# Retention head outputs and gates laid with tokens on partitions, normed per token, then turned

## The reference, cut to what matters

```python
q, k, v, g = split(h @ w_in, [1024, 2048, 4096])      # widths 1024, 1024, 2048, 2048
q, k = rotary(q), rotary(k) * 256 ** -0.5
# per head: scores (256 x 256) times decay ** |distance|, a decay for each direction, times v
o = o_fwd + o_bwd                                      # (token, head, 512)
mu  = mean(o, axis=-1);  var = mean((o - mu) ** 2, axis=-1)
o = ((o - mu) * rsqrt(var + 1e-6)).reshape(b, s, 2048) * gn_g
return (silu(g) * o) @ w_out                           # 2048 -> 1024
```

## Time and profile before

| | us |
|---|---|
| median of three runs | 1710.88 |
| the profiled execution | 1711.01 |
| its span, first to last instruction | 1708.9 |
| PE matmul busy | 1640.0 (96%) |
| PE weight load busy | 1492.4 (87%) |
| DVE busy | 1258.7 (74%) |
| ACT busy | 897.9 (53%) |
| mean granted TensorE clock | 0.982 of 2.4 GHz |
| retention stage, projections, within the trace | 988.9 to 1126.2 |
| retention stage, heads and output chunks | 1126.2 to 1216.4 |

### The profile page before, as it was taken

One profiled execution on the slowest core, in us unless ns is written; L12 is line 12 of the kernel. 1 busy time (PEld: TensorE's weight loads), 2 busy tenths in 40 slices (PEclk: granted clock), 3 DMA queues, 4 the chain that ended last, 5 costly groups with the idle time before them and its releaser, 6 DMA issues.

```text
span 1708.9 us, 28898 instructions
## 1 busy us (share of the span) xinstructions
PE 1640.0 (96%) x10694; PEld 1492.4 (87%) x10694; DVE 1258.7 (74%) x1868; ACT 897.9 (53%) x1165; POOL 42.1 (2%) x50
## 2 busy tenths in 40 slices
PE   8988999989799999999999999998999999799998
PEld 8877999968699999878999998987899997699997
DVE  5765878767688787875877775448787786878777
ACT  5474544554665455564554554444554555555453
POOL 0000000000000000000000042000000000000000
PEclk9999999989899999999999999999999999899999
DMA  7353454434464544422545455522455454445543
GB/s 277 102 181 133 175 193 179 189 126 169 148 246 174 195 176 169 173 100 95 195 170 203 170 178 195 175 96 89 169 195 203 169 191 173 148 148 197 196 172 123
DMA packets 42148, 288.61 MB, mean 169 GB/s; under 512 B 4929, under 2 KB 5057, under 8 KB 8673
## 3 DMA queue, kind: packets, MB, share of 16 engines
q1 hardware_dynamic: 40000, 278.62, 44.6%
q0 software_dynamic: 2080, 9.05, 1.5%
HBM read 286.61 MB, written 1.05 MB: 168 GB/s over the span
## 4 chain that ended last, share of the span: by engine, by line
PE 83%; DVE 10%; ACT 3%; issue 2%; DMA 1%; DVEq 0%; SPq 0%; ACTq 0%
PE bank L1721 15%; PE bank L1723 15%; PE bank L1722 15%; PE bank L1815 7%; PE bank L1816 7%; PE bank L1817 7%; PE bank L1767 3%; PE bank L1769 3%; PE bank L1768 3%; DVE w_lo L989 2%; PE bank L1708 1%; DVE arena L1262 1%; ACT w_hi L533 1%; PE bank L1864 1%; PE bank L1843 1%
## 5 line engine op out<-in xcount | busy, mean ns | idle before, releaser
L1721 PE MATMUL bank<-h_hi,w_hi 128*128 128x256 f32 x2368 | 680.9, 288 | 18.6 <-issue 9.9
L1722 PE MATMUL bank<-h_hi,w_lo 128*128 128x256 f32 x2368 | 674.6, 285 | 0.0
L1723 PE MATMUL bank<-h_lo,w_hi 128*128 128x256 f32 x2368 | 674.6, 285 | 0.0
L1721 PEld LDWEIGHTS bank<-h_hi,w_hi 128*128 128x128 f32 x2368 | 456.2, 193 | 28.1 <-issue 17.5
L1722 PEld LDWEIGHTS bank<-h_hi,w_lo 128*128 128x128 f32 x2368 | 456.3, 193 | 4.6 <-issue 1.4
L1723 PEld LDWEIGHTS bank<-h_lo,w_hi 128*128 128x128 f32 x2368 | 456.2, 193 | 1.0
L989 DVE TENSOR_TENSOR w_lo<-raw,w_hi 128x2048 fp32r<-128x2048 f32 (+3 forms) x119 | 249.1, 2101 | 118.0 <-ACT w_hi L533 117.7
L1289 DVE TENSOR_TENSOR w_lo<-raw,w_hi 128x2048 fp32r<-128x2048 f32 x145 | 327.5, 2285 | 1.6 <-ACT w_hi L729 1.6
L717 ACT ACTIVATE arena<-arena,par 128x256 f32<-128x256 f32 x220 | 120.4, 595 | 357.9 <-DVE arena L1248 354.7
L729 ACT ACTIVATE w_hi<-raw 128x2048 fp32r<-128x2048 f32 x150 | 286.0, 1907 | 19.7 <-PE bank L1817 19.7
L1815 PE MATMUL bank<-w_hi,h_hi 128*128 128x512 f32 x632 | 249.3, 395 | 3.7 <-DVE w_lo L989 2.2
(11 more groups left out here) (184 smaller groups left out, 1296.3 us busy)
## 6 DMA issues: line engine op xcount, KB each, us to landing
raw<-wstream SPq DMA_DIRECT2D x258, 1024.0 KB, 4.8
arena<-window_bias POOLq DMA_DIRECT2D x4, 768.0 KB, 6.8
arena<-dilated_bias POOLq DMA_DIRECT2D x8, 256.0 KB, 3.3
arena<-conv_rows POOLq DMA_DIRECT2D x2, 1024.0 KB, 5.9
raw<-wstream SPq DMA_DIRECT2D x4, 384.0 KB, 3.3
raw<-wstream SPq DMA_DIRECT2D x6, 256.0 KB, 3.1
x<-x_in SPq DMA_DIRECT2D x1, 1024.0 KB, 4.8
raw<-wstream SPq DMA_DIRECT2D x2, 512.0 KB, 6.6
```

What stands on the lines that cost most here:

```text
L1721: nc.tensor.matmul(dst, w_parts[0], x_parts[0], start=start, stop=False, **kw)
L1722: nc.tensor.matmul(dst, w_parts[1], x_parts[0], start=False, stop=False, **kw)
L1723: return nc.tensor.matmul(dst, w_parts[0], x_parts[1], start=False, stop=stop, **kw)
```

## The change

Gates become `token_chunk` products like the values, and `value_evac` applies Silu with the scale per token on ACT; `by_root` and the in-place Silu are gone for them. An output has tokens on partitions. The statistics come from `bn_stats` and `bn_aggr` along the free axis, the root is on 128 x 2 columns, ACT writes `(o - mean) * root` into SBUF, DVE multiplies by the gate, PE transposes the result into the head's two banks (`turn_head`), and ACT and DVE take `h_hi` and `h_lo` from there with the gain. All four heads' decays are computed beside chunks 8 to 11. `mean` and `var` are gone, and the orders of PE, ACT and DVE are new.

```diff
-    for c in range(16, 24):
-        split_hi(c0 + c + 2)
-        g = pair(g_r, c - 16)
-        act.wait_ge(evac_v, k["ev"] + c - 15)
-        nc.scalar.activation(g, g, ACT.Silu).then_inc(evac_done, 1)
+    for c in range(8, 24):                                    # ACT
+        split_hi(c0 + c + 2)
+        if 8 <= c < 12:
+            act.wait_ge(mask_v, 2 * (c - 8) + 2)
+            nc.scalar.activation(d_r[:, c - 8, :], d_r[:, c - 8, :], ACT.Exp).then_inc(mask_a, 1)
+        if c % 2:
+            n = (c - 9) % 8 // 2
+            value_evac(c0 + c - 1, (v_r if c < 16 else g_r)[:, :, n * 512:(n + 1) * 512],
+                       func=ACT.Copy if c < 16 else ACT.Silu)
+    def head_norm(h):
+        act.wait_ge(v_ready, k["v"])
+        nc.scalar.activation(r_y[:, h, :], r_v[:, h, :], ACT.Abs_reciprocal_sqrt).then_inc(ars_done, 1)
+        act.wait_ge(ret_root, h + 1)
+        for j in range(2):
+            nc.scalar.activation(o_tok(h, j), o_bank(h, j)[:, :], ACT.Identity, bias=r_b[:, h, j:j + 1],
+                                 scale=r_y[:, h, j:j + 1]).then_inc(ret_normal, 1)
+    def head_parts(h):
+        for n in range(2):
+            act.wait_ge(ret_turned, 2 * h + n + 1)
+            for t in range(2):
+                slot = 4 * h + 2 * n + t
+                nc.scalar.activation(h_hi[:, slot, :], o_bank(h, n)[:, t * S:(t + 1) * S], ACT.Identity,
+                                     scale=pcol("ret_gn_g_2", slot)).then_inc(hhi_done, 1)
+    split_hi(c0 + 26); head_norm(0); head_norm(1); head_parts(0); head_parts(1); head_norm(2)
+    head_parts(2); split_hi(c0 + 27); head_norm(3); head_parts(3)
+    for c in range(28, 34): split_hi(c0 + c)
...
+    def stats(h):                                             # DVE
+        for j in range(2):
+            dve.wait_ge(ret_out, 2 * h + j + 1)
+            nc.vector.bn_stats(y_st[:, j, h, :], o_bank(h, j)[:, :]).then_inc(ret_stats, 1)
+    def head_root(h):     # two bn_aggr, var + eps, wait for ACT's root, three Newton steps, -mean * root
+    def head_gate(h):
+        for j in range(2):
+            dve.wait_ge(ret_normal, 2 * h + j + 1)
+            nc.vector.tensor_tensor(o_tok(h, j), o_tok(h, j), g_r[:, j, h * 512:(h + 1) * 512], ALU.mult)
+    def head_parts(h):    # four scalar_tensor_tensor: o_bank * gain - h_hi into h_lo
+    for c in range(8, 24):
+        if c < 12: decays(c - 8)
+        split_lo(c0 + c + 2)
+    probs(0); probs(1); stats(0); head_root(0); stats(1); head_gate(0); probs(2); head_root(1)
+    probs(3); head_gate(1); head_parts(0); stats(2); head_parts(1); head_root(2); head_gate(2)
+    split_lo(c0 + 26); stats(3); head_root(3); head_parts(2); head_gate(3)
+    split_lo(c0 + 27); head_parts(3)
+    for c in range(28, 34): split_lo(c0 + c)
...
+    def output(h):                                            # PE
+        pe.wait_ge(prob_done, 4 if h == 3 else h + 1)
+        for j in range(2):
+            for jt in range(2):
+                at = jt * S + j * P
+                last = nc.tensor.matmul(o_bank(h, j)[:, :], p_r[:, h % 2, at:at + P],
+                                        v_r[:, jt, h * RVD:(h + 1) * RVD], start=jt == 0, stop=jt == 1)
+            last.then_inc(ret_out, 1)
+    def turn_head(h):     # waits ret_gated 2h + 2; eight transposes, ret_turned after each four
+    score(0); score(1); output(0); output(1); score(2); score(3); turn_head(0); output(2)
+    turn_head(1); output(3); project(0); project(1); turn_head(2); project(2); project(3)
+    turn_head(3); project(4); project(5); project(6); project(7)
```

More of the change, by code:

```diff
@@ L581, in evac, with value_evac @@
                 k["evac"] += 1
-            def value_evac(c, dst, scaled=True, heads=None):
+            def value_evac(c, dst, scaled=True, heads=None, func=ACT.Copy):
                 for j in range(2):
@@ L595, in value_evac @@
                     if scaled:
-                        ins = nc.scalar.activation(to, values, ACT.Copy, scale=tok_y[:, j:j + 1])
+                        ins = nc.scalar.activation(to, values, func, scale=tok_y[:, j:j + 1])
                     else:
@@ L931, in head_out @@
[L931 to L958, removed]
@@ L962, in _ @@
+                    head_norm(0)
                     head_norm(1)
-                    split_hi(c0 + 26)
+                    head_parts(0)
+                    head_parts(1)
+                    head_norm(2)
+                    head_parts(2)
                     split_hi(c0 + 27)
[L965 to L968, removed]
                     head_norm(3)
-                    for c in range(30, 34):
+                    head_parts(3)
@@ L971, in _ @@
+                    for c in range(28, 34):
                         split_hi(c0 + c)
-                    k["sum"] = sum0 + 2 * len(RET_SUMS)
-                    k["centred"] += 8
                 k["x"] += 4
@@ L1023, in root, with normalize @@
                 dve.wait_ge(newton, k["newton"])
-            def normalize(sources, times=None, by_root=True):
+            def normalize(sources, by_root=True):
                 def lo(i):
@@ L1042, in normalize @@
                         first = nc.vector.tensor_scalar(hn[:, slot, :], view, gain, None, ALU.mult)
[L1043 to L1049, removed]
+                    first.then_inc(hn_done, 1)
                     k["hhi"] += 1
@@ L1628, in _, with decays @@
                         nc.vector.tensor_tensor(halves(rot[:, 2 * (c % 2) + 1, :]), src, sin2, ALU.mult).then_inc(rot_v, 1)
[L1629 to L1636, removed]
+                    def decays(h):
+                        d = d_r[:, h, :]
                         if h >= 2:
-                            dve.wait_ge(prob_done, h - 1)
+                            dve.wait_ge(rot_p, 16)
                         nc.vector.tensor_scalar(d, cc("fwd", 512), G_[:, h:h + 1], None, ALU.mult).then_inc(mask_v, 1)
@@ L1679, in _ @@
+                    head_parts(0)
+                    stats(2)
+                    head_parts(1)
+                    head_root(2)
+                    head_gate(2)
                     split_lo(c0 + 26)
+                    stats(3)
+                    head_root(3)
+                    head_parts(2)
+                    head_gate(3)
                     split_lo(c0 + 27)
-                    head_norm(2)
-                    split_lo(c0 + 28)
-                    split_lo(c0 + 29)
-                    head_norm(3)
@@ L2118, in mean @@
-                    def mean(h):
-                        if h:
-                            pe.wait_ge(mean_read, h)
-                        for e in range(2):
-                            pe.wait_ge(evac_done, k["evac"] + 2 * h + e + 1)
-                            for n in range(2):
-                                last = nc.tensor.matmul(bank[2][:, 0:S], ones, o_ret(h, 2 * e + n), start=e + n == 0, stop=e + n == 2)
-                            last.then_inc(sum_done, 1)
-                    def var(h):
-                        sum_squares([512] * 2)
+                                at = jt * S + j * P
```

150 lines of the change are left out of this document (73 added, 77 removed).

## The result

The changed kernel took 1695.29 us (median of 4 runs, 1694.05 to 1696.32) against 1707.84 for the one before beside it (4 runs, 1704.58 to 1712.01): a ratio of 0.9921, 95% interval 0.9901 to 0.9941. Later runs of the same kernel gave 0.9936 [0.992, 0.9953]. So it is faster, by 0.64 to 0.79%; the medians stand 12.6 us apart beside the result and 10.3 in the later runs. The direction and the place of every wait were right. The gain was forecast too small, by about half against that median, and the time lies in the forecast's range (1694.5 to 1709) near its lower end.

The account below looks back on a forecast made before the run. PE, busy in 96% of the span, was taken as the bound. Gates -2.53 us and the rest of the stage from 90.28 to 83.55 (-6.7) gave -9.3 from the profiled 1711.01: 1701.7 us, range 1694.5 to 1709.

Parts of the forecast that it names:

- Gates and first wait: Gate chunks cost what value chunks do, -2.53 us; the wait before the first score falls from 1.61 to 0.84.
- PE's work in the heads: Means and variance sums removed, about 13.4 us; transposes added, 3.74; scores and outputs unchanged: 9.7 us less.
- rival B: Turning the heads on PE is dear: 0.27 us or 0.39 per transpose, 1706.6 to 1710.4 us; chance 0.07.
- A: Heads dearer: slow `bn_stats` from PSUM, 512-column matmuls not fully overlapped, a gap ahead of `project(0)`; 1707 us, chance 0.16.
- The seams: Where one kind of PE matmul follows another in the stage, 0.8 us is lost, as before the change.
- The order of the heads: Retention stage's instruction order: no wait up to `project(0)` at 23.4 us, then PE waits of 4.1 and 5.6 us.
- gap 1: PE's wait for split weights ahead of `project(3)`, the fourth output chunk: 4.1 us.
- gap 2: PE's wait for split weights ahead of `project(4)`, the fifth output chunk: 5.6 us.
- The clock in the gaps: PE at half clock after the two gaps loses 1.75 and 2.5 us, 4.25 in all, all of it paid.
- Rival C: The two gaps are there but the clock holds, or they are shorter: 1697.4 us; chance 0.15.
- D: PE stays at 1.2 GHz from gap 1 through the last five projections, losing 28 us: 1725.5 us; chance 0.04.
- E: Weights wait for the heads so much that gaps swallow the saving: about 1711 us; chance 0.05.

Follow-up runs that it names:

- gates_only: The kernel before with only the eight gate chunks as token chunks and Silu on the way out of the bank; 1705.27 us, ratio 0.9988 to the kernel before.
- order_both: The changed kernel with weight splits of chunks 27, 28 and 29 ahead of the parts of heads 2 and 3 on ACT and DVE; 1690.57 us, ratio 0.9891.
- order_gap2: The changed kernel with only chunk 28's weight split put ahead of head 3's parts, on ACT and DVE; 1688.50 us, ratio 0.9894 to the kernel before.
- after_look3: The changed kernel unchanged, profiled a fourth time; 1696.41 us.
- after_again: The changed kernel run again unchanged; 1696.93 us (6 runs), ratio 0.9936 to the kernel before; its profiled execution took 1702.4.
- order_gap1: The changed kernel with only chunk 27's weight split and head 3's norm ahead of head 2's parts; 1692.29 us, ratio 0.992 to the kernel before.

## Why the prediction was right and where it failed

The stage was to fall by 9.26 us and fell by 13.14. What failed are sizes, not the mechanism: the price of the clock in the gaps first, then the gaps' length and the seams, and the execution that the forecast was hung on.

**Gates and first wait: right.** Forecast -2.53 and -0.77, together -3.3. The time to the first score fell by 3.2, in gates_only too. From the gates' end to the first score it is 0.94 (1120.22 to 1121.16), forecast 0.84.

**PE's work in the heads: right in kind, 1.1 short.** Outputs of 512 columns cost what those of 256 did, as argued from the sums' durations. The turns took 3.3 in all (0.87, 0.87, 0.79, 0.79 in order_both, where no gap follows a turn) for 3.74 forecast, so rival B fell (0.27 for each transpose, or the 390 ns that the Trainium skill gives for a bf16 one in VectorE: DVE Perf Modes, The three transpose paths). This trace has 0.10 to 0.11 us for each float32 one, eight in a row. `bn_stats` of 512 from PSUM took 0.70 (forecast 0.65), so A fell too: no wait of an output, no gap ahead of `project(0)`. Without gaps and clock the rest went from 88.67 - 6.6 - 3.4 = 78.7 to 67.85, by 10.8 where 9.7 was forecast. 0.4 of the 1.1 is the turns; the other 0.7 are seams, next.

**The seams: failed, 0.9 with the turns.** The forecast carried 0.8 us over from the stage before, by measured less worked out. The gapless rest is 67.85, and the bookkeeping without seams had been 82.75 - 0.84 - 9.7 - 4.25 = 67.96. With the turns at their measured length that is 67.5, which leaves 0.3 for seams. The leftover of the stage before holds the restarts after its two long gaps too, some 0.5 each if they are as in order_gap2, so part of what was called seams may have been gaps; no run took the gap of 4.4 away.

**The order of the heads: right.** Gaps of 3.41 and 5.34 us for 4.1 and 5.6, where and why it said: ACT idle 9.85 and 9.76 for the turns (10 forecast), DVE behind ACT's root. The order kernels show the cause. The gaps were forecast 0.95 too long. Of that 0.56 is the chain of gap 1, from the first rounded part of turn 2 to PE's start, 9.27 us (1155.22 to 1164.49) for 9.83: DVE's four small steps and two gates take 0.66 and 1.20 for 0.8 and 1.38, ACT's four parts and its split 1.44 and 1.81 for 1.54 and 1.90. The chain of gap 2 was right, 5.75 for 5.8. The prediction calls the chunk behind the old gap of 2.2 us the sixth output chunk; it is the seventh, c = 30, and nothing in the sum hangs on it.

**The clock in the gaps: failed, and the largest term of the stage's miss.** Forecast 4.25 us. Three of four executions show 2.1 to 2.3 with the restart (1.7 to 1.8 by the clock alone), the fourth 5.5. "Gap 1 is between the two of this stage, each with 3.5 us at the lower level" took one profile's rows for the price of a gap. It isn't a price. Of half clock on a busy PE the gap of 2.2 us had 3.4 us or none behind it, that of 3.4 none or 5.7, that of 4.4 had 3.4 or 6.1, and that of 5.3 had 3.3 to 4.7, in the same kernel from one execution to the next. "All of it paid" failed too: in after_look3 half of a slow stretch lay in the gap itself and cost nothing. Rival C (the clock holds) described gap 1 in the profile shown and not gap 2. D (no return to full clock through the projections) fell: the longest slow stretch at a gap is 6.8 us. Even so after_again has 10.5 us of slow work behind its two gaps together.

**The baseline: failed.** "It is 0.13 above the median, so it stands for it" rested on three runs. Over 22 runs made beside the experiments the kernel before has a median of 1707.1; the profiled 1711.01 was a high one. The same stage saving taken from 1707.1 would have given 1697.8, against measured medians of 1695.29 and 1696.93. Of the 14.7 us between the two profiled executions the stage gives 13.14. The work ahead of the stage, which the change doesn't touch, gives 3.38 (986.76 to 983.38; 37.6 us at the lower level there before, 27.3 after), and the work behind it takes 1.82 back (492.41 to 494.24). The forecast's -9.26 for the stage fell 3.9 short: 2.1 by clock and restart, 0.95 by the gaps and 0.9 by seams and turns, less 0.1 for the first wait. The rest of the distance from 1701.7 to the profiled 1696.3 is these stretches elsewhere, 1.56. Nearly all of the 1.82 is the loss of 1.7 by one stretch of 3.4 us at the lower level far behind the change, where the profile before has none:
```profile
1413.00:1420.00 7.00, 7.00 (x20) 4.53 (x19) 2.65 (x3) 2.52 (x4) 0.00 (x0) 0.76 0.58 198
```

**E, the gaps swallow the saving: fell, but held most of what was left.** Gaps and their clock cost 10.9 us, nearly as much as the change saves (13.14). order_both, with a stage of 205.66 for 216.54 and 229.68 before, is the better kernel: 0.9891 [0.9869, 0.9913] of the one before. order_gap2, on another chip, can't be told from it by its times (0.9894), though its stage is 3.9 longer: by then the stretches in other stages weigh more than the gap.

## What to carry to other kernels

When steps on two engines change places with a transpose on the third, write out each engine's list and look for work that needs nothing standing behind an instruction that waits: here it cost 8.75 us of waiting, and moving it ahead gave that back, 10.9 us of the stage with the clock and 6.4 in the median time. Take the price of a wait on a TensorE-bound path as its length plus a spread for the clock (here 0 to 3 us each), not as a number from one profile. Anchor a forecast at the median of many runs and add the difference of the stage, not at the execution that happened to be profiled.

## What the runs showed of the hardware

What the clock costs behind a wait differs from one execution to the next. The same kernel with the same waits to 0.02 us lost 2.1 to 2.3 us to the clock and the restart in the stage in three executions and 5.5 in a fourth, and a gap of 3.41 us was followed by full clock (32 records in 6.5 us) or by clock 0.57 (17 in 6.7). What sets this is not shown here.

Over the whole trace the stretches at the lower level add to 52.5 us in the changed kernel's profile of 1696.32 us and to 66.8 in that of 1702.4. Half of the difference is 7.1 us, and the times are 6.1 apart, most of the spread of its six later runs (1694.26 to 1702.4). Some of these stretches lie where TensorE doesn't wait (375 to 379 us, clock 0.58 in one execution and 1.00 in another). A stretch that begins inside a gap costs only what of it falls on work: in order_gap1 6.8 us at half clock cost 1.8.

A gap of 3.41 us with full clock on both sides cost 4.0, 0.54 more than its length (order_gap2). Float32 transposes of 128x128 stand 0.10 to 0.11 us apart when eight follow each other.

The TensorE page of the Trainium skill (TensorE: Matmul & The Clock Gate, HAM oscillation) tells of a kernel that waits for DMA between bursts and has 1.67 us throttled for each wait, half of it lost. In the changed kernel's profile it was 3.4 us and 1.7 after gap 2, and nothing after gap 1.
